# Second mixer on VectorE: scores, logits and sums ahead of the fills' low parts of weights, and the residual's scaling ahead of the value units' low part

## The reference, cut to what matters

```python
h = rms_norm(x, mix_norm_gain)
q_a, k_a, v_a, q_b, k_b, v_b, gate_logits = split(h @ w_in)
y_a = sliding_window_sink_attention(q_a, k_a, v_a, q_gain, k_gain, sinks)
y_b = stick_breaking_attention(q_b, k_b, v_b)
gates = sigmoid(gate_logits + gate_bias)
merged = gates[0] * (y_a @ w_up_swa) + gates[1] * (y_b @ w_up_sb)
x = x + merged @ w_out
x = x + peer_ffn(rms_norm(x, ffn_norm_gain), ...)

# stick-breaking, per head: z = q k^T / 8, before = key < query
log_keep = where(before, log_sigmoid(-z), 0)
suffix = reverse_cumsum(log_keep) - log_keep
weights = where(before, exp(log_sigmoid(z) + suffix), 0)
```

## Time and profile before

| | |
|---|---|
| median of 3 runs | 1924.19 us (1919.99 to 1926.89) |
| the profiled execution's own time | 1920.3 us |
| its span | 1918.5 us |
| TensorE matmuls busy | 1757.7 us, 92% of the span |
| TensorE weight loads busy | 1394.3 us, 73% |
| VectorE busy | 1292.6 us, 67% |
| ScalarE busy | 913.2 us, 48% |
| GpSimd busy | 318.3 us, 17% |
| mean granted TensorE clock | 0.989 |

### The profile page before, as it was taken

The page is one execution under the profiler, slowest core; times in us unless marked ns, Lnnn a source line. Parts: engine busy times, 40 slices in busy tenths (PEclk is TensorE's granted clock), DMA queues, the critical chain, the costliest instruction groups (busy, mean ns, idle before and its releaser), DMA issues.

```text
span 1918.5 us, 29208 instructions
## 1 busy us (share of the span) xinstructions
PE 1757.7 (92%) x11218; PEld 1394.3 (73%) x11218; DVE 1292.6 (67%) x2402; ACT 913.2 (48%) x1901; POOL 318.3 (17%) x331
## 2 busy tenths in 40 slices
PE   9999999999999999899999889989987787777777
PEld 8999979999999999589999779975432232222222
DVE  5565897556765675976557766875876766766544
ACT  5444565444544453764445455634544344344343
POOL 1000003000000000030000000433433333333331
PEclk9999999999999999999999999999999999999999
DMA  7555435975555545135555333689999999999997
GB/s 292 186 178 197 139 99 152 266 251 178 172 192 195 180 152 181 44 111 191 194 180 172 125 109 121 208 328 387 405 421 421 422 421 422 421 421 421 422 421 314
DMA packets 96138, 485.02 MB, mean 253 GB/s; under 512 B 10576, under 2 KB 10832, under 8 KB 62976
## 3 DMA queue, kind: packets, MB, share of 16 engines
q0 software_dynamic: 38544, 275.25, 37.3%
q1 hardware_dynamic: 57456, 207.90, 32.4%
HBM read 478.65 MB, written 4.46 MB: 252 GB/s over the span
## 4 chain that ended last, share of the span: by engine, by line
PE 56%; DMA 15%; DVE 12%; issue 9%; POOL 4%; ACT 3%; another core or an unknown queue 0%; POOLq 0%; SPq 0%; ACTq 0%; DVEq 0%
PE PS L548 15%; PE PS L550 15%; PE PS L549 15%; PE PS L2243 3%; DVE WL L1038 2%; DMA WH<-uv,A 2%; DMA XF<-uv,A 2%; DMA YL<-uv,A 2%; DMA raw<-uv,A 2%; DMA YH<-uv,A 2%; PE PS L2264 2%; DMA raw<-wst 2%; ACT WH L669 1%; POOL raw L652 1%; DMA XH<-uv,A 1%
## 5 line engine op out<-in xcount | busy, mean ns | idle before, releaser
L1038 DVE TENSOR_TENSOR WL<-raw,WH 128x1024 fp32r<-128x1024 f32 (+1 forms) x375 | 449.8, 1241 | 95.4 <-ACT WH L669 95.1
L548 PE MATMUL PS<-XH,WH 128*128 128x256 f32 x1616 | 459.4, 284 | 4.7 <-DVE XL L1046 1.9
L550 PE MATMUL PS<-XH,WL 128*128 128x256 f32 x1616 | 455.0, 282 | 0.0
L549 PE MATMUL PS<-XL,WH 128*128 128x256 f32 x1616 | 455.0, 282 | 0.0
L669 ACT ACTIVATE WH<-raw 128x1024 fp32r<-128x1024 f32 (+1 forms) x375 | 370.8, 1041 | 45.4 <-PE PS L550 18.8
L548 PEld LDWEIGHTS PS<-XH,WH 128*128 128x128 f32 x1616 | 305.5, 189 | 7.8 <-issue 3.3
L549 PEld LDWEIGHTS PS<-XL,WH 128*128 128x128 f32 x1616 | 305.4, 189 | 0.2
L550 PEld LDWEIGHTS PS<-XH,WL 128*128 128x128 f32 x1616 | 305.1, 189 | 0.0
L981 ACT ACTIVATE A<-A,RTK 128x1 f32<-128x1 f32 x256 | 75.0, 293 | 298.8 <-DVE A L1664 297.2
L722 ACT ACTIVATE A<-A 128x256 f32<-128x256 f32 x88 | 36.8, 418 | 342.4 <-DVE A L1073 342.4
L548 PE MATMUL PS<-GH,WH 128*128 128x256 f32 x704 | 198.2, 282 | 1.1 <-DVE WL L1038 1.1
(11 more groups left out here) (316 smaller groups left out, 2947.8 us busy)
## 6 DMA issues: line engine op xcount, KB each, us to landing
raw<-wst SPq DMA_DIRECT2D x381, 512.0 KB, 4.6
raw<-wst SPq DMA_DIRECT2D x8, 384.0 KB, 3.7
vscr<-A POOLq DMA_DIRECT2D x1, 3072.0 KB, 38.8
A<-vscr POOLq DMA_DIRECT2D x1, 2048.0 KB, 22.8
C<-cst SPq DMA_DIRECT2D x1, 1236.5 KB, 10.4
raw<-uv,A POOLq DMA_INDIRECT x65
hT<-xin SPq DMA_DIRECT2D x2, 512.0 KB, 4.9
A<-vscr POOLq DMA_DIRECT2D x1, 1024.0 KB, 12.7
```

What stands on the lines that cost most here:

```text
L548: pe.matmul(o, wh, xh, start=start, stop=False, skip_group_check=True)
L549: pe.matmul(o, wh, xl, start=False, stop=False, skip_group_check=True)
L550: return pe.matmul(o, wl, xh, start=False, stop=stop, skip_group_check=True)
L1038: dv.tensor_tensor(WL[:, m % SPL, 0:w], raw[:, i % RAW, 0:w], f32(WH[:, m % SPL, 0:w]), ALU.subtract).then_inc(s_lo, 1)
```

## The change

VectorE's program alone is touched; nothing is added or removed. The 8 scalings of `hT` go ahead of `lo("va", 0)`. In steps 0 to 6 `low_out`, `scores` and `logits` go ahead of the low pair; in steps 7 and 10 `log_weight`, in step 8 `logits`. `low_out` also moves from behind `normalise` to the head of its step.

```diff
--- before.py
+++ after.py
@@ -1381,12 +1381,12 @@
             dv.wait_ge(s_used, U("va", 0))
             dv.scalar_tensor_tensor(out=VT, in0=PS[:, 4, 0:T], scalar=1.0, in1=RT[:, 1, :], op0=ALU.mult,
                                     op1=ALU.mult).then_inc(s_vt, 1)
-            lo("va", 0)
 
             for kc in range(8):
                 ins = dv.scalar_tensor_tensor(out=hT[:, kc, :], in0=hT[:, kc, :], scalar=c("gains", 48 + kc, 49 + kc),
                                               in1=RT[:, 0, :], op0=ALU.mult, op1=ALU.mult)
             ins.then_inc(s_hf, 1)
+            lo("va", 0)
             dv.wait_ge(s_qrs, 1)
             own(dv.reciprocal(RS, RS))
             own.wait()
@@ -1514,29 +1514,29 @@
                 low_out(YL, YH, 4 + p, 6 + p % 2, O_SB + p)
 
             for i in range(7):
-                rest = fill()
+                if i >= 3:
+                    low_out(YL, YH, i - 3, 6, O_SWA + i - 3)
                 if i < 4:
                     scores(i)
-                if 1 <= i < 5:
-                    normalise(i - 1)
-                if i >= 3:
-                    low_out(YL, YH, i - 3, 6, O_SWA + i - 3)
                 if i == 5:
                     logits(0)
                     logits(1)
+                rest = fill()
+                if 1 <= i < 5:
+                    normalise(i - 1)
                 if i == 6:
                     softplus(0)
                     softplus(1)
                 rest()
-            rest = fill()
             log_weight(0)
             log_weight(1)
+            rest = fill()
             weight(0)
             weight(1)
             rest()
-            rest = fill()
             logits(2)
             logits(3)
+            rest = fill()
             sb_low(0)
             sb_low(1)
             rest()
```

## The result

The change takes 1903.28 us (median of 4, 1902.60 to 1904.34), before 1922.67 (median of 4, 1919.99 to 1926.89). The ratio is 0.9899, 95% interval 0.9887 to 0.9911: 19.4 us less, 1.0%. A second job gave 1903.16 (4 runs) against 1922.26 (9 runs), ratio 0.9898 (0.9883 to 0.9913).

What follows compares the result with a forecast made beforehand. In the second mixer no engine was full: TensorE waited for VectorE, which waited for ScalarE's high parts. Gains summed to 16.7 us, minus 0.7 for hand-overs: 16 less, 1908.2 against the median (1904.3 profiled); range 1903.5 to 1916.

Steps and rivals of the forecast that it cites:

- the loop through ScalarE: Second mixer's steps: VectorE waits for ScalarE's high parts before scores, 9.4 us a step; without it 7.44 us.
- Part one: Value units: residual's 8 scalings moved ahead of va's low parts, into VectorE's idle time; 4.9 us gained.
- Dates of the steps: Second mixer: R with a number is the end of that step's rest, freeing bank 7; gains reach 16.7 us.
- The new waits for low_out: Steps 3 to 6: VectorE waits for ScalarE ahead of low_out, 1.3 to 1.8 us each.
- The 0.7 us taken off for hand-overs: Over the steps: about ten hand-overs between engines, under 0.1 us each, taken off the 16.7 us gain.
- The step that failed: from the profiled execution to the median: Whole kernel: 16 us less gives 1904.3 for the profiled execution's 1920.3, and 1908.2 against the median of 1924.19.
- the slow stretches: TensorE at low clock: 1.7 us at value units, 3 allowed with 1107.70 to 1118.20's neighbours; 18.6 bound with idle time.
- VectorE's round trip: Rival, steps 3 to 6: the wait scores lost returns ahead of low_out; 8.6 us less, 1915.6; chance 0.13.
- Bank 7's hand-over: Rival, fills 0 to 6: fills tied to rest, only value units gain; 4.9 us less, 1919.3; chance 0.05.
- Work after the stage: Rival, after 1187 us: something else, such as weight loads, holds that work; within 0.3%; chance 0.05.
- No fill waited for a low part: Rival, TensorE's fills: low parts come too late; 20.9 us more, 1945; chance 0.03.

Runs made afterwards that it cites:

- scores_ahead_only: Changed kernel with low_out, logits and log_weight back where they were before; scaling and scores stay ahead. 1908.56 us (5 runs), ratio to before 0.9927.
- all_but_scores: Changed kernel with scores put back behind the low pair in steps 0 to 3. 1909.33 us (5 runs), ratio to before 0.9933.
- before_seventh: The kernel before, unchanged, profiled once more; stage 138.08 us, mean clock 0.75 from 1140 to 1150 us.
- normalise_ahead: Changed kernel with normalise also ahead of the low pair and low_out behind scores and normalise. 1901.75 us (4 runs), against 1903.16 for the change.

## Why the prediction was right and wrong

- **What bounds the stage, and the loop through ScalarE**: right. VectorE's waits for WH went from 20.3 to 1.0 us, the step from 9.4 to 7.34 us (7.44 worked out). scores_ahead_only and all_but_scores show that both halves are needed.
- **Part one**: right. TensorE's wait is 0.25 us (0.3 said), the 12 matmuls take 2.99 us (2.8 said). By the spacing that the Trainium skill gives for 512-column matmuls ("TensorE: Matmul & The Clock Gate", section "Wait — 56ns, not 53.3ns?"), a dozen at full clock is 2.6 us, an estimate; the trace has 2.99 from the first one's start to the next group's, and decides.
- **Dates of the steps**: with the later entry of 0.6 us taken off, R1 and R2 fell on 1091.7 and 1099.05 (1091.7 and 1099.1 said), R3 on 1108.0 (1108.3), R4 on 1114.8 (1115.2), R6 on 1132.2 (1132.7), the second suffix sums on 1154.0 (1154.7). The new waits for low_out were 1.23, 1.28, 1.83 and 1.14 us (1.3 to 1.8 said); those of steps 3 and 6 were a little too long in my working. So the stage lost 17.4 against before's entry, not 16.7.
- **The 0.7 us taken off for hand-overs**: wrong. The durations between starts in the rows hold the hand-overs already. This and the point above are the 1.4 us between 16 and 17.4.
- **The step that failed: from the profiled execution to the median.** The forecast for the profiled execution was 1904.3 us, and the changed kernel's took 1903.47, off by 0.8. The forecast for the median was 1908.2, and 1903.28 was measured, off by 4.9. The other 4.1 us lie in "with 1920.3 at the low end of the runs; against the median it is 1908.2": that set the same 16 us against 1924.19 and so carried the 3.9 us by which before's median stood above its profiled execution over to the changed kernel. Its median stands 0.2 us below its own profiled execution. Of the 3.9 us, 1.5 were the chance of three runs (1922.67 with the fourth); the other 2.4 are the distance of that median from the profiled execution.
- **The term that was mis-sized: the slow stretches**, 1.7 us at the value units and "with the stretch's neighbours I allow 3. Together 18.6", which set the lower end of the range. They were read off one execution, and for that one the 4.7 us are right (TensorE's busy time fell by 4.8). But TensorE's clock behind the 3.02 us wait was 1.00 in it, and I took that as a property of the kernel. In four of before's eight profiled executions it fell there, and the stage took 0.9 to 2.6 us more. The mean of TensorE's busy time over the eight is 5.8 us above the change's, in before_seventh alone 7.8. The mean of the eight stages is 136.2 us, that of the change 118.0: 18.2 us.
- **What stays open**: 18.2 lies inside the interval of the ratio (17.1 to 21.7 us), so the clock places 0.7 of the 1.9 us between the first profile's 17.5 and the medians' 19.4; the last 1.2 us isn't placed. What was not tried is a profile of each timed run.
- **Rivals**: VectorE's round trip happened as a wait (5.5 us in four places) but cost only the 1.35 us that normalise_ahead gets back. Bank 7's hand-over didn't bind: the rule of the Trainium skill on rotating PSUM banks ("Perfetto Trace Analysis", section "Matmuls") names a hand-over that exists here (before, TensorE waited 0.7 us for rest once); in the changed kernel TensorE's values and transposes fill it, and no wait of TensorE for rest is left. Work after the stage kept its length (56.47 and 56.48 us). No fill waited for a low part.

## What to carry to other kernels

In a program of engines in strict order, work that is needed late (here the low parts, with 5 us of cover) belongs behind work that another engine's long answer hangs on; look for one engine's wait that stands in front of work which doesn't need it. Work the dates out from starts in the trace and take nothing off for hand-overs. And where idle times of TensorE of 2 to 3 us are removed, profile the kernel before more than once, price the low clock behind them by the mean, and forecast the median from medians: the kernel gets steadier as well as shorter, so the distance between one profile and the median doesn't carry over.

## What of the hardware was not expected

The same idle time of TensorE, 3.01 to 3.03 us ahead of the first suffix sums, was followed by the clock at 2.4 GHz in four profiled executions of before and by 1.2 GHz in the other four, which made the sums 1.4 to 2.8 us longer (the first two matmuls took 0.70 us and 1.22 us). And 16 unread matmuls put into waits made a kernel with more work 3.4 us faster (0.9983, 0.9974 to 0.9992); with six more the spread of its 11 runs was 2.7 us, where 21 runs of before spread over 6.9.
